# A ring of 19 expert places, the last down matrix one expert at a time, and a closing norm shared between VectorE, TensorE and ScalarE

## What is computed

```python
x = _layer_norm(DEEPNORM_ALPHA * x + mixed, ln1_g[l], ln1_b[l])
# _hier_moe(x): combine[token, expert] holds the two router weights of a token, else 0
h = silu(einsum('td,edf->etf', xt, w_gate)) * einsum('td,edf->etf', xt, w_up)
h = h * combine.T[:, :, None]
ffn = einsum('etf,efd->td', h, w_down)
...
x = _layer_norm(DEEPNORM_ALPHA * x + ffn, ln2_g[l], ln2_b[l])
# _layer_norm: (xf - mu) * rsqrt(var + 1e-5) * g + b
```

## Time and profile before

| what | value |
|---|---|
| median of 3 runs | 1341.87 us (1341.77 to 1343.75) |
| profiled execution, its own time | 1344.68 us |
| its span | 1342.5 us |
| TensorE busy | 1311.3 us, 98% |
| VectorE, ScalarE busy | 584.2 us, 483.3 us |
| read from HBM | 361.95 MB |

### The profile page before, as it was taken

The page is one execution under the profiler, slowest core; times in us unless marked ns, Lnnn a source line. Parts: engine busy times, 40 slices in busy tenths (PEclk is TensorE's granted clock), DMA queues, the critical chain, the costliest instruction groups (busy, mean ns, idle before and its releaser), DMA issues.

```text
span 1342.5 us, 17750 instructions
## 1 busy us (share of the span) xinstructions
PE 1311.3 (98%) x7285; PEld 965.2 (72%) x7285; DVE 584.2 (44%) x757; ACT 483.3 (36%) x671; POOL 28.2 (2%) x49
## 2 busy tenths in 40 slices
PE   9999999999999999999999999999999999999894
PEld 8999989998888888888888888744354443544442
DVE  4387444546545645454555554615122021220207
ACT  4454344436465544454333433412121121211211
POOL 1000000400000000000100000000000000000000
PEclk9999999999999999999999999999999999999998
DMA  9767555545444445554556795799999999999995
GB/s 302 257 197 262 174 188 189 188 158 181 164 148 165 156 141 185 190 172 157 187 187 231 271 381 185 277 380 357 423 421 421 421 421 422 421 421 421 421 407 225
DMA packets 120462, 364.95 MB, mean 272 GB/s; under 512 B 11529, under 2 KB 17097, under 8 KB 96337
## 3 DMA queue, kind: packets, MB, share of 16 engines
q1 hardware_dynamic: 114080, 359.58, 72.1%
q10 hardware_dynamic: 6320, 4.49, 1.1%
HBM read 361.95 MB, written 2.10 MB: 271 GB/s over the span
## 4 chain that ended last, share of the span: by engine, by line
PE 89%; DMA 8%; DVE 2%; SPq 1%; ACT 0%; issue 0%; DVEq 0%
PE main L1119 19%; PE main L1121 19%; PE main L1120 19%; PE main L520 13%; PE att L591 6%; DMA mraw<-in_expert_w_down_dram 5%; PE att L474 4%; DMA mraw<-in_expert_w_up_dram 2%; PE att L1368 1%; DMA raw<-in_w_in_dram 1%; PE main L486 1%; PE main L487 1%; PE att L1351 1%; PE att L1387 1%; PE att L1383 1%; PE att L1338 0%
## 5 line engine op out<-in xcount | busy, mean ns | idle before, releaser
L1785 DVE TENSOR_TENSOR wlo<-raw,whi 128x2048 fp32r<-128x2048 f32 x134 | 308.1, 2299 | 353.9 <-ACT whi L1534 353.9
L1534 ACT ACTIVATE whi<-raw 128x2048 fp32r<-128x2048 f32 x134 | 256.1, 1912 | 413.5 <-PE main L1121 410.6
L520 PE MATMUL main<-mraw,xg 128*64 128x512 f32 x1024 | 225.5, 595 | 1.1 <-DMA mraw<-in_expert_w_up_dram 1.0
L1119 PE MATMUL main<-whi,xhi 128*128 128x512 f32 (+1 forms) x544 | 203.8, 375 | 0.0
L1121 PE MATMUL main<-whi,xlo 128*128 128x512 f32 (+1 forms) x544 | 201.7, 371 | 0.0
L1120 PE MATMUL main<-wlo,xhi 128*128 128x512 f32 (+1 forms) x544 | 201.5, 370 | 0.0
L520 PEld LDWEIGHTS main<-mraw,xg 128*64 128x64 f32 x1024 | 72.1, 137 | 137.1 <-issue 135.9
L1119 PE MATMUL main<-xhi,whi 128*128 128x256 f32 (+1 forms) x560 | 159.5, 285 | 1.0 <-DVE wlo L1917 0.5
L1120 PE MATMUL main<-xlo,whi 128*128 128x256 f32 (+1 forms) x560 | 158.4, 283 | 0.0
L1121 PE MATMUL main<-xhi,wlo 128*128 128x256 f32 (+1 forms) x560 | 158.4, 283 | 0.0
L1121 PEld LDWEIGHTS main<-whi,xlo 128*128 128x128 f32 x544 | 102.5, 188 | 17.6
(11 more groups left out here) (331 smaller groups left out, 1340.3 us busy)
## 6 DMA issues: line engine op xcount, KB each, us to landing
raw<-in_w_in_dram SPq DMA_DIRECT2D x95, 1024.0 KB, 5.0
mraw<-in_expert_w_gate_dram SPq DMA_DIRECT2D x64, 1024.0 KB, 19.1
mraw<-in_expert_w_up_dram SPq DMA_DIRECT2D x64, 1024.0 KB, 20.6
mraw<-in_expert_w_down_dram SPq DMA_DIRECT2D x64, 1024.0 KB, 17.3
raw<-in_w_branch_dram SPq DMA_DIRECT2D x24, 1024.0 KB, 5.1
raw<-in_w_out_dram SPq DMA_DIRECT2D x16, 1024.0 KB, 6.5
xin<-in_x_dram SPq DMA_DIRECT2D x4, 512.0 KB, 8.3
out_dram<-out_acc SPq DMA_DIRECT2D x8, 256.0 KB, 2.0
```

Of the source, the lines that this page charges most:

```text
L520: ins = pe.matmul(main[0][half, w, :], xg[:, k, half], src[:, kk * DE:(kk + 1) * DE], start=(k == 0), stop=(k == KT - 1))
L1119: pe.matmul(o, ah, bh, start=start, stop=False, skip_group_check=skip)
L1534: act.activation(whi[:, u % SPLIT, 0:n], raw[:, slot, 0:n], ACT.Copy).then_inc(hi_done, 1)
L1785: dve.tensor_tensor(wlo[:, u % SPLIT, 0:n], raw[:, slot, 0:n], whi[:, u % SPLIT, 0:n].bitcast(F32), ALU.subtract).then_inc(lo_done, 1)
```

## The change

**The ring.** The two places that held `l2g` and `l2b` (they lie where `l1g` and `l1b` are in use until `acc_ok`) become places 20 and 21 of the weights, and the router's place 19 joins as well: the ring has 19 places. The first pass over the ring (`second_round`) has 17 places, then units 41 and 42 are the first ones in places 20 and 21 and wait for `acc_ok` in place of `m_used`. `l2g` and `l2b` now go into ring places that fall free in the last pair, behind a wait for seven of its units.

**The last down matrix.** Each piece's four products of expert 0 run together, and then the four of expert 1. Each half waits for its own unit alone. The scatter of the piece before stands between the two halves.

**The closing norm.** Five of the eight blocks (Z = 5) are finished by TensorE and ScalarE: TensorE puts the bias into a PSUM bank (a product of a row of ones with a row of `l2b`), and adds the product of a diagonal matrix `dg` of `rstd` with the centred block; ScalarE copies the bank to `out_acc`. ScalarE makes the two `dg` matrices from the identity. VectorE still centres all eight blocks and finishes the last three. `final_adds` on VectorE takes the low part of piece 1 behind the adds of block 0. The blocks leave in the order 0, 1, 2, 5, 3, 6, 4, 7.

```diff
-MRAW = 16
+MRAW = 19
+Z = 5
+STEPS = 2 * GROUP
...
-        l2g, l2b = at("l2g", made["khT"], [P, D]), at("l2b", made["qst"], [P, D])
...
+        NP = len(places)
+        places += [made["khT"], made["qst"]]
         mraw = [at(f"mraw{j}", o, [P, UNIT]) for j, o in enumerate(places)]
-        NP = len(places)
-        ring = [j for j in range(NP) if j not in once and j != router_place]
+        second_round = [j for j in range(NP) if j not in once]
+        GROWN = NP + len(second_round)
+        ring = second_round[:4] + [NP, NP + 1] + second_round[4:]
         assert len(ring) == MRAW

         def place(g):
-            return g if g < NP else ring[(g - NP) % MRAW]
+            if g < NP:
+                return g
+            return second_round[g - NP] if g < GROWN else ring[(g - GROWN) % MRAW]
...
+        L2R = MU - MRAW
+        l2g, l2b, ysb = (at(n, places[ring[(LAST0 + L2R + j) % MRAW]], [P, D]) for j, n in enumerate(("l2g", "l2b", "ysb")))
...
             for g in range(NP, FIRST * MU):
-                sp.wait_ge(m_used, user_before(g) + 1)
+                if user_before(g) is None:
+                    sp.wait_ge(acc_ok, 1)
+                else:
+                    sp.wait_ge(m_used, user_before(g) + 1)
                 load_unit(sp, g % MU, g // MU, place(g))
...
-            sp.wait_ge(acc_ok, 1)
+            sp.wait_ge(m_used, turns * MU + FIRST * MU + L2R + 2)
             for dst, name in ((l2g, "ln2_g"), (l2b, "ln2_b")):
...
-                    for d, (c, c0, w) in enumerate(pieces):
+
+                    def down(d, a):
+                        c, c0, w = pieces[d]
+                        src, landed_, value = unit(4 * QUADS + 2 * c + a)
+                        half = slice(a * SLOTS, (a + 1) * SLOTS)
+                        pe.wait_ge(landed_, value)
+                        for f in range(DE // P):
+                            ins = pe.matmul(y_of(d)[half], hT[:, f, half], src[:, f * 512 + c0:f * 512 + c0 + w],
+                                            start=(f == 0), stop=(f == DE // P - 1), skip_group_check=True)
+                        if a == 1:
+                            ins.then_inc(y_ps, 1)
+
+                    for d in range(3):
                         if d == 2:
                             pe.wait_ge(sc_free, 1 + m * 8)
-                        for a in range(2):
-                            _, landed_, value = unit(4 * QUADS + 2 * c + a)
-                            pe.wait_ge(landed_, value)
-                        for f in range(DE // P):
-                            for a in range(2):
...
+                        down(d, 0)
                         if d:
                             last_scatter(d - 1, m)
-                    last_scatter(len(pieces) - 1, m)
+                        down(d, 1)
+                    down(3, 0)
+                    down(4, 0)
+                    last_scatter(2, m)
+                    down(3, 1)
+                    down(4, 1)
+                    last_scatter(3, m)
+                    last_scatter(4, m)
+                    pe.wait_ge(l2_in, 32)
+                    for z in range(Z):
+                        pe.matmul(norm_bank(z), ones[0:1, :], l2b[0:1, blocks[z][1]], start=True, stop=False)
+                    pe.wait_ge(l2_std, 2)
+                    for z in range(Z):
+                        t, cols = blocks[z]
+                        pe.wait_ge(centred, z + 1)
+                        pe.matmul(norm_bank(z), dg[:, t, :], out_acc[:, t, cols], start=False, stop=True).then_inc(o_ps, 1)
                     return
...
             act.activation(rstd[:], bag[:, :, 1], ACT.Sqrt).then_inc(l2_std, 1)
+            act.wait_ge(l2_var, 2)
+            for t in range(T):
+                ins = act.activation(dg[:, t, :], ident[:], ACT.Copy, scale=rstd[:, t:t + 1])
+            ins.then_inc(l2_std, 1)
+            for z in range(Z):
+                t, cols = blocks[z]
+                act.wait_ge(o_ps, STEPS + z + 1)
+                act.activation(out_acc[:, t, cols], norm_bank(z), ACT.Copy).then_inc(o_hi, 1)
...
-                low_part(0, m)
-                for c in (1, 2):
+                for c in range(3):
                     low_part(c, m)
-                    final_add(c - 1, m)
+                    if c < 2:
+                        final_add(c, m)
...
                 if n == 1:
                     dve.wait_ge(l2_std, 1)
-                    link(dve.reciprocal(rstd[:], rstd[:]))
-                if n:
+                    dve.reciprocal(rstd[:], rstd[:]).then_inc(l2_var, 1)
+                if n > Z:
                     second(n - 1)
             second(len(blocks) - 1)
...
-            for n, (t, cols) in enumerate(blocks):
-                sp.wait_ge(out_ok, n + 1)
+            for n in (0, 1, 2, 5, 3, 6, 4, 7):
+                t, cols = blocks[n]
+                if n < Z:
+                    sp.wait_ge(o_hi, STEPS + n + 1)
+                else:
+                    sp.wait_ge(out_ok, n - Z + 1)
                 sp.dma_start(out[0, t * P:(t + 1) * P, cols], out_acc[:, t, cols]).then_inc(out_done, 16)
```

More of the change, by code:

```diff
@@ L246, in build @@
         places.append(made["sig"])
+        NP = len(places)
+        places += [made["khT"], made["qst"]]
         mraw = [at(f"mraw{j}", o, [P, UNIT]) for j, o in enumerate(places)]
-        NP = len(places)
-        ring = [j for j in range(NP) if j not in once and j != router_place]
+        second_round = [j for j in range(NP) if j not in once]
+        GROWN = NP + len(second_round)
+        ring = second_round[:4] + [NP, NP + 1] + second_round[4:]
         assert len(ring) == MRAW
         def place(g):
-            return g if g < NP else ring[(g - NP) % MRAW]
+            if g < NP:
+                return g
+            return second_round[g - NP] if g < GROWN else ring[(g - GROWN) % MRAW]
         def user_before(g):
-            return max(e for e in range(g) if place(e) == place(g))
-        LOOP0, LAST0 = (FIRST * MU - NP) % MRAW, (FIRST * MU + MU - NP) % MRAW
-        ysb = at("ysb", places[ring[(LAST0 + MU - MRAW) % MRAW]], [P, D])
+            return max((e for e in range(g) if place(e) == place(g)), default=None)
+        LOOP0, LAST0 = (FIRST * MU - GROWN) % MRAW, (FIRST * MU + MU - GROWN) % MRAW
+        L2R = MU - MRAW
+        l2g, l2b, ysb = (at(n, places[ring[(LAST0 + L2R + j) % MRAW]], [P, D]) for j, n in enumerate(("l2g", "l2b", "ysb")))
         small = [made["ksT"], made["pT"]]
@@ L268, in build @@
         hh, hT = carve(0, "hh", [P, DE]), carve(0, "hT", [P, DE // P, 2 * SLOTS])
+        dg = at("dg", made["ksT"], [P, T, P])
         hot, cmb = carve(0, "hot", [P, T, 2 * SLOTS]), carve(0, "cmb", [P, T, 2 * SLOTS])
@@ L337, in build @@
             "moe_const pair_done sel_ok eg_in eg_out ed_in ed_out pos_ps np_ok")
-        shared = [(U1 + 10 + j - 6) % RAW if 6 <= j < 6 + RAW else None for j in range(NP)]
-        mlanded = [sem(f"mlanded{j}") if shared[j] is None else landed[shared[j]] for j in range(NP)]
+        shared = [(U1 + 10 + j - 6) % RAW if 6 <= j < 6 + RAW else None for j in range(len(places))]
+        mlanded = [sem(f"mlanded{j}") if shared[j] is None else landed[shared[j]] for j in range(len(places))]
         mbase = [0 if i is None else 16 * sum(1 for u in range(1, U1 + 4 * QUADS) if u % RAW == i) for i in shared]
@@ L428, in scattered, with norm_bank @@
             return main[1][:, n % 2, :] if n < 6 else att[:, n - 4, :]
+        def norm_bank(z):
+            return att[:, z, :] if z < 4 else main[0][:, 1, :]
         def keep_warm(pe, n):
@@ L574, in step @@
-                        ins.then_inc(y_ps, 1)
+                        down(d, 0)
                         if d:
                             last_scatter(d - 1, m)
-                    last_scatter(len(pieces) - 1, m)
+                        down(d, 1)
[6 more added lines that the diff above has]
+                    last_scatter(4, m)
@@ L877, in second @@
                 t, cols = blocks[n]
+                dve.wait_ge(l2_var, 2)
                 dve.wait_ge(centred, n + 1)
```

## The result

| what | before | after |
|---|---|---|
| median | 1342.84 us (20 runs) | 1345.13 us (20 runs) |
| lowest to highest | 1341.62 to 1344.23 | 1342.56 to 1348.65 |
| profiled execution, own time and span | 1344.68, 1342.5 us | 1343.42, 1341.2 us |

The ratio of after to before is 1.0020, 95% interval 1.0014 to 1.0027: +2.7 us (+1.9 to +3.6). The forecast was +2.3, the time forecast 1344.2 us. The total is right, and by luck: two of the three terms that make it are not, a term of +9.6 us was +4.5, and one of -2.9 was +0.9.

The account below looks back on a forecast made before the run. Transfers were taken to bound the kernel, with a TensorE and VectorE chain behind the last unit. Ring -4.4, down stage +9.6 and norm -2.9 sum to +2.3 us on the 1341.87 us median: 1344.2 us, bounds 1342.0 to 1347.6.

Parts of the forecast that it names:

- The bound: Experts' part: transfers at 420 GB/s set the end; TensorE has 7.4 us of slack, so earlier transfer stops count.
- The ring: Weight transfers: stops at 933 us (3.5 us) and 922 us (0.9 us) go, together -4.4 us; bounds 3.5 and 4.6.
- The last down matrix: Last down stage: records of one expert run alone at 0.434 us, stage 30.0 us in place of 20.4, +9.6 us.
- the last record of one and the first of the other run side by side: Last down stage, where experts change with nothing between: one record overlaps, giving back 1.5 us of 27.8.
- My lower bound of +8.6: Last down stage: least cost expected, where the forecast was +9.6 us and the upper bound +10.8.
- The closing norm: End of the kernel: work shared with TensorE and ScalarE ends the span 10.5 us after first centring, not 13.4: -2.9 us.
- the last is issued at about B + 8.0 and lands 2.3 later or a little more: Output transfers: last issue 8.0 us after the first centring pass starts, landing 2.3 us later or slightly more.
- the stage of 30 us: Sign for the last down stage: about 30 us to the first L498, with no wait for a unit.
- the clock of 1.00: Sign for the closing norm: TensorE stays at granted clock 1.00, since the new products keep it at work.
- the 10.5 us of the norm: Sign for the closing norm: 10.5 us from the start of the first centring pass to the end.
- Rival 4: Closing norm: granted clock falls ahead of the rstd products, 8.7 in place of 4.3 us, +4.4, 1348.6 us; chance 0.05.
- Rival 2: Last down stage: lone record takes 0.343 us, stage 24.6 us, +4.2; sum -3.1, 1338.8 us; chance 0.05.

Follow-up runs that it names:

- ring_alone: Changed kernel with the last down stage and closing norm put back as before, leaving only the ring of 19 places: 1339.05 us, 0.9976 of the kernel before.
- full_row_bias: Changed kernel with the norm's bias from a product of the identity with all 128 bias rows, not one row: 1342.03 us, 0.9997 of the kernel before.
- ring_norm: Changed kernel with down products alternating again; ring, shared norm and one-row bias products stay: 1341.95 us, 0.9992 of the kernel before.

## Why the prediction was right, and which steps were not

**The bound.** Right. Transfers at 421 GB/s set the pace, TensorE had slack, and what the ring freed at 925 us arrived at the last stage.

**The ring: -4.4 forecast, -4.0 measured** (424.0 for 428.0 us in the profiles; -3.2 by the ratio and -3.5 by the medians of ring_alone). Right in mechanism and, within 0.4 us, in size. Adding the two stops was right for the whole ring, since it leaves none; for a ring of 17, where I expected 3.4 us by the same sum, it was not (2.6). In the profile of ring_alone 0.8 us of the gain went again inside the last stage, which waited 3.0 us for units in place of 2.3 and took 21.1 us in place of 20.4.

**The last down matrix: +9.6 forecast, +4.5 measured.** The direction and its cause were right: records of 0.434 us run alone where they ran in pairs, the last two pieces take 1.8 us for eight records of one expert, and the units had all landed. The step that failed is "the last record of one and the first of the other run side by side", 1.5 us given back. Four records of the busy half do so at each change: three changes between runs of 512 columns give 3 x 4 x 0.434 = 5.2 us, and at the change from 512 to 256 columns the eight short records of expert 0 start beside the last four long ones, 1.7 us. 27.8 - 6.9 + 3.8 = 24.7, and the stage is 24.8. My row, the alternating stream, could not show this: a reach of one record and of four look alike in it. My lower bound of +8.6 had no row behind it, and +4.5 lies far outside.

**The closing norm: -2.9 forecast, +0.9 measured.** The passes were priced right (last copy at B + 7.5 with the clock held, 7.7 in the sum). Two things were not. First the clock: I had it as a rival with 0.05 and argued that TensorE stays at work, so that the clock stays at 1.00. TensorE does stay busy, with one row of weights, and the clock is 0.50 from 1329.5 to 1332.5 all the same. That is 1.9 us in the profile. Second the end: "the last is issued at about B + 8.0 and lands 2.3 later or a little more". I did note four transfers within 1.4 us, and did not work out the rate: with the clock held all eight are issued in under 5 us, 2.1 MB takes 5.6 at 374 GB/s, and the longest time to landing grows from 2.3 to 3.8 us. Another 1.9 us (12.45 for 10.5, in full_row_bias).

**The sum.** +2.3 forecast, +2.7 by the ratio. The errors of -5.1 and +3.8 us nearly cancel, and that is luck: both terms lie outside their own bounds, and of the signs that I named the stage of 30 us, the clock of 1.00 and the 10.5 us of the norm all failed. The four rivals would each have been off. Rival 4 named the right mechanism at the right place, and came together with a down stage that cost half. Rival 2 forecast a stage of 24.6 us, as good as the 24.8 measured, but for another reason: it has a lone record at 0.343 us, and the loads above come 0.43 apart while one half runs alone. The length of the stage couldn't have told the two apart.

**What stays open.** The parts measured alone, -3.5, +4.9 and +2.9 us by the medians, make +4.3, and the whole is +2.3 to +2.7. The down order is the term that moves: +4.9 alone (+4.8 by the ratio, with an interval from +3.1 to +6.7), 3.2 by the medians and 3.8 by the ratios with ring and norm in place (the changed kernel against ring_norm), 3.3 and 4.0 with the full-row bias. In the profiles the same three comparisons of the stage give 4.5, 4.5 and 4.4 us. So the gap lies within the noise of the medians, and I don't settle it. Nor is it known why the clock was low for longer in some executions than in others.

## What to carry to other kernels

Products that use one half of TensorE should change halves at least every four records, as far as fp32 records of 512 columns show it; grouping them by operand to start on the first one that lands buys the wait and pays with the pairing. Work that is put on TensorE to fill its idle time is better done with all rows: here the time was the same and the clock was held. And where the last engine's work is split in two to end sooner, first divide the output's bytes by the rate at which they can leave, and start that stream early.

## What the runs showed that I had not expected

- TensorE starts on the free half once four records of the busy half are left, out of turn: eight records of one expert followed by eight of the other take 5.25 us, runs of four 3.53, strict alternation 3.48.
- One-row products of full length didn't keep the granted clock: it fell to 0.50 while they ran or just behind them, with TensorE busy, in the changed kernel and in ring_norm (bias records from 1322.20 on, 0.50 in the window from 1326.0 to 1332.0); with all rows it stayed at 1.00 through the norm in the three kernels that have them. One row took no less time, 3.69 us for eight against 3.60.
- The Trainium skill (TensorE: Matmul & The Clock Gate, Part 3, The mechanism) says that matmuls start and end strictly in order. This case's trace doesn't agree on the start: 24 records of 0.434 us on alternating halves in 7.1 us need starts out of that order.
- Ahead of the experts, identical code varied by 2.8 us between profiled executions, more than the effect under test; only stretches measured from their own start could be compared.
